# A two-layer macaron transformer trunk: where the row scale factors are spread over the partitions

## The chip, the cores and the metric

One Trainium2 chip, one of its NeuronCores. The metric is the device time of one launch in microseconds (us). Engines: PE (TensorE), DVE (VectorE), ACT (ScalarE), POOL (GpSimd), SP (SyncE, here only a queue of DMAs).

## The reference, cut to what matters

`x` is 256 tokens by 1024 features, float32. There are two layers; each is a half-step SwiGLU feed-forward (FFN), a token mixing (eight heads of sparse latent attention with an indexer and a top-64, and eight heads of forgetting attention) and a second half-step FFN:

```
for l in range(2):
    h = h + 0.5 * swiglu(rms_norm(h, ffn1_norm[l]), ffn1_gate[l], ffn1_up[l], ffn1_down[l])
    h = h + token_mixing(rms_norm(h, mix_norm[l]), w_in[l], ...)
    h = h + 0.5 * swiglu(rms_norm(h, ffn2_norm[l]), ffn2_gate[l], ffn2_up[l], ffn2_down[l])
return rms_norm(h, final_norm)
```

`rms_norm` divides each token (row of `h`) by the root of its mean square, then multiplies by a gain per feature. `swiglu(x) = (silu(x @ w_gate) * (x @ w_up)) @ w_down`, with 2816 hidden features. There are thus six normalizations inside the layers (numbered n = 0 to 5 below: n = 0, 2, 3 and 5 stand before an FFN, n = 1 and 4 before a mixing) and a seventh at the end.

## The kernel before, in words

The tokens lie as two blocks `b` of 128 on the partitions (`X`). Each block is transposed on PE (16 transposes a norm, L674), so that features lie on the partitions and tokens along the free dimension; ACT multiplies by the gain and rounds to the high part `xhi`, DVE makes the low part `xlo`. Each float32 product is made from high and low parts of both operands, in matmuls of 128x512 and 128x256. The weights come as a stream of chunks (3 units of 1024 columns each: the "front" of two units, in an FFN gate and up, and the "back" of one unit, down). SP loads them into two slots of `raw` (L246 front, L250 back) as soon as the slot's chunk before has been split; ACT rounds them to `whi`, DVE subtracts to get `wlo` (L1065, L1071; a few of these on POOL).

The row factor of a norm is not applied to `x`. The matmuls run on the gained, unnormalized `x`, and their output, which has features on the partitions and tokens along the free dimension, is multiplied by `rows`, a tile of 128 partitions by 256 tokens, in which every partition holds the same 256 row factors. It is used by DVE and, in the mixing, by POOL.

How `rows` comes about, for each of the six norms: ACT sums squares per token (L379), DVE makes the mean (`mean`, L1082), POOL raises to the power -0.5 (`power`, L297, one instruction for each block, into `rstd`, one factor per partition). DVE multiplies the identity by `rstd` into two diagonals of 128x128 (L1112). PE multiplies a matrix of ones by the two diagonals into a PSUM bank (`spread_rows`, which calls `spread`, L682), in the middle of the gate tile of the second chunk (FFN: `up(1)`) or of the first query tile (mixing: `tile(QI)`). DVE copies the bank to `rows` (L1118) and goes on. Order on DVE in `norm` (L1085): the eight `xlo`, mean of block 0, split of the first front half of the next chunk, mean of block 1, two diagonals, split of the second half, the copy.

Order on DVE behind it: in an FFN (`step(0)`) `hg` = gate * rows (L1136), `ur` (L1144), then ACT's sigmoid, `ht` (L1147), `hf` (L1159), ACT's rounding to `hhi` (L415) and `hlo` (L1161). PE's order is written out by hand: `up(0)`, `up(1)`, `down(0)`, then `up(2)`, `down(1)` and so on; `down(0)` waits for `hlo` (L729). In the mixing DVE first does `ct` = latent * rows (L1252), a copy of the small weights' projection (`wft`, L1254), the index key (L1256, two halves), the split of the back of chunk 1 (L1071), ten small operations, and, after POOL's `crstd` (L347), two diagonals for a second spread (L1276); PE does `tile(QI)`, then `tile(QI + 1)` with `token_major` (L863 and L868, which waits for `wft` and for ACT's square of `ct`) in its middle, then `tile(QI + 2)` with `latent_rows` in its middle, which spreads the latent's own factors in the same way as before (`spread`, L682) and isn't touched by the change.

All waits are semaphores set by hand; every engine runs its own instructions in order.

Of the kernel before, what the change touches and what calls it, by code (L numbers as in the profile page):

```python
# [17 lines left out]
F32 = mybir.dt.float32  # L18
F32R = mybir.dt.float32r
BF16 = mybir.dt.bfloat16  # L20
ALU = mybir.AluOpType
ACT = mybir.ActivationFunctionType

P = 128
D = 1024
S = 256
# [56 lines left out]

def trunk(nc, x, stream, gains, final_gain, consts, rel_bias, out, table):
    with ExitStack() as ctx:
# [3 lines left out]
        def sems(names):  # L89
            return [ctx.enter_context(nc.semaphore(n)) for n in names.split()]  # L90
# [83 lines left out]

        ROWS_FFN, ROWS_MIX = 2, 7
        CB = 2
# [25 lines left out]
        front_done, back_done = sems("front_done back_done")  # L202
        x_ready, ss_out, ms_out, rstd_out, diag_out, rows_mm, rows_out = sems(
            "x_ready ss_out ms_out rstd_out diag_out rows_mm rows_out")
        ones_set, nc2_set, pickr_set, ur_out, ht_out, nchi_out = sems("ones_set nc2_set pickr_set ur_out ht_out nchi_out")
# [82 lines left out]
        def _(pool):  # L288
# [4 lines left out]
            def power(n):  # L293

                for b in range(NB):
                    pool.wait_ge(ms_out, n * NB + b + 1)
                    nc.gpsimd.tensor_tensor(rstd[:, b:b + 1], ms[:, b:b + 1], mhalf[:, b:b + 1],  # L297
                                            ALU.pow).then_inc(rstd_out, 1)

            def split_front(l, m, half):  # L300

                k = NF + m
                s, at = k % 2, slice(half * UNIT, (half + 1) * UNIT)
                pool.wait_ge(w_front, chunk(l, k) * 2 + half)
                pool.wait_ge(hi_front, chunk(l, k) * 2 + (half + 1))
                nc.gpsimd.tensor_tensor(wlo[:, s, at], raw[:, s, at], whi[:, s, at].bitcast(F32),
                                        ALU.subtract).then_inc(w_front, 1)
# [32 lines left out]
            for l in range(DEPTH):  # L340
                power(l * 3)
                power(l * 3 + 1)
                if l == 0:
                    pool.wait_ge(const_in, 16)
                    nc.gpsimd.tensor_copy(pickr[:], pick).then_inc(pickr_set, 1)
                pool.wait_ge(cms_out, l + 1)
                nc.gpsimd.tensor_tensor(crstd[:, :], cms[:, :], mhalf[:, :], ALU.pow).then_inc(crstd_out, 1)  # L347
                split_front(l, 4, 0)
                scale(l, 0, 1)
                split_front(l, 4, 1)  # L350
                scale(l, 1, 2)
                split_back(l, 4)
                scale(l, 2, 3)
                split_front(l, 5, 0)
                scale(l, 3, 4)
                split_front(l, 5, 1)
                scale(l, 4, NWIDE)
                for hh in range(2 * NH):
                    share(l, hh)
                power(l * 3 + 2)  # L360
            power(DEPTH * 3)

# [234 lines left out]
        def _(pe):  # L597
# [86 lines left out]

            def spread_rows(n, bank):

                pe.wait_ge(diag_out, n + 1)
                spread(bank).then_inc(rows_mm, 1)

            def ffn(l, phase):  # L690
                k0 = phase * (NF + MIXC)

                def up(f, i=0):
# [15 lines left out]
                    for g in range(2):  # L709
# [6 lines left out]
                        for k in range(KT):  # L716
                            if f == 1 and g == 0 and k == KT // 2:
                                spread_rows(l * 3 + 2 * phase, ROWS_FFN)
                            if f == NF - 1 and g == 1:
                                t = three(ps[:, GU + 2 * s + 1, 0:S], w(s, UNIT + k * P, P), xt(k), k == 0, k == KT - 1)  # L720
                            else:
                                t = wide(GU + 2 * s + g, w(s, g * UNIT + k * P, P), k)
# [31 lines left out]
            def mix(l):  # L754
# [126 lines left out]
                u.then_inc(feat_mm, 1)  # L881
                tile(QI, front(1, 0), 0, lambda: spread_rows(l * 3 + 1, ROWS_MIX))
                tile(QI + 1, front(1), UNIT, token_major)
# [175 lines left out]
        def _(dve):  # L1059
# [24 lines left out]

            def norm(n, g, l, k, bank, first=False):  # L1085

# [21 lines left out]
                if not first:  # L1108
                    mean(n, 1)
                for b in range(NB):  # L1110
                    dve.wait_ge(rstd_out, n * NB + b + 1)
                    t = nc.vector.tensor_scalar(diag[:, b, :], ident, rstd[:, b:b + 1], None, ALU.mult)  # L1112
                t.then_inc(diag_out, 1)
                split_front(l, k, halves=(1,))
                if first:
                    split_back(l, 0)
                dve.wait_ge(rows_mm, n + 1)
                nc.vector.tensor_copy(rows[:, :], ps[:, bank, 0:S]).then_inc(rows_out, 1)  # L1118
                dve.wait_ge(rows_out, n + 1)

# [268 lines left out]
            for l in range(DEPTH):  # L1389
                norm(l * 3, G_FFN1, l, 1, ROWS_FFN, first=l == 0)  # L1390
                ffn(l, 0)
                norm(l * 3 + 1, G_MIX, l, NF + 1, ROWS_MIX)
                mix(l)
                norm(l * 3 + 2, G_FFN2, l, NF + MIXC + 1, ROWS_FFN)
                ffn(l, 1)
# [109 lines left out]
```

## Time and profile before

| what | value |
|---|---|
| median of 3 runs | 1011.92 us (1011.25 to 1012.65) |
| the profiled execution's own time | 1012.57 us |
| its span, first to last instruction | 1010.7 us |
| PE, DVE, ACT, POOL busy | 997.6, 763.0, 538.5, 124.7 us |
| granted TensorE clock, mean | 0.997 of full speed |

Times in rows are microseconds from the span's start; a row of a timeline is start, duration, engine, line, operation, output<-inputs, shapes, count, and in brackets how long the engine was idle just before and what ended that. The duration of a matmul is from issue to its modelled end, and matmuls overlap; what one adds to PE's time is read from the starts or from the chain.

### The profile page before, as it was taken

The numbers are of one execution on the slowest core, as the hardware profiler recorded it, in microseconds if no ns is written. First come the engines' busy times: TensorE is split into PE (matmuls) and PEld (weight loads), VectorE is DVE, ScalarE is ACT, GpSimd is POOL, SyncE is SP. The second block draws the span as 40 slices with busy tenths as digits, with TensorE's granted clock in tenths as the row PEclk, the third lists the DMA queues.
The fourth block names the chain that finished last, engine by engine and source line by source line (L and its number), as shares of the span: only waits on it lengthen the run. The fifth ranks groups of instructions, "written<-read, shape, count | busy, mean of one in ns | idle before, by whom it ended". The sixth has DMA issues, their size and how long they took to land.

```text
span 1010.7 us, 16529 instructions
## 1 busy us (share of the span) xinstructions
PE 997.6 (99%) x5652; PEld 846.2 (84%) x5652; DVE 763.0 (75%) x1556; ACT 538.5 (53%) x974; POOL 124.7 (12%) x148
## 2 busy tenths in 40 slices
PE   9999999999999999999999999999999999999996
PEld 8878888898878888888888888889887788888885
DVE  6868777688677877777788777777786778777775
ACT  5545555566556555555555555555755555555552
POOL 1000000018552000000000000000185400000000
PEclk9999999999999999999999999999999999999998
DMA  8786556544525665555536555554363446555541
GB/s 319 223 277 208 190 185 189 184 160 137 205 68 182 194 221 187 186 187 187 188 126 211 187 188 188 187 187 149 137 213 121 164 152 219 194 187 187 187 145 42
DMA packets 36053, 183.17 MB, mean 181 GB/s; under 512 B 3984, under 2 KB 6192, under 8 KB 21680
## 3 DMA queue, kind: packets, MB, share of 16 engines
q1 hardware_dynamic: 35632, 182.53, 54.6%
q8 instruction: 23, 0.38, 0.2%
q10 hardware_dynamic: 384, 0.15, 0.1%
q14 instruction: 14, 0.11, 0.0%
HBM read 181.61 MB, written 2.62 MB: 182 GB/s over the span
## 4 chain that ended last, share of the span: by engine, by line
PE 93%; DVE 3%; DMA 2%; ACT 1%; issue 1%; POOL 0%; POOLq 0%; DVEq 0%; SPq 0%; ACTq 0%
PE ps L606 31%; PE ps L607 16%; PE ps L600 12%; PE ps L602 12%; PE ps L601 12%; DMA raw<-stream 2%; PE ps L839 1%; PE ps L616 1%; DVE wlo L1065 1%; PE ps L674 1%; PE ps L620 1%; PE ps L617 1%; PE ps L851 1%; PE ps L830 1%; PE ps L826 1%
## 5 line engine op out<-in xcount | busy, mean ns | idle before, releaser
L606 PE MATMUL ps<-xboth,whi 128*128 128x512 f32 x1440 | 508.5, 395 | 1.5 <-DVE wlo L1065 1.5
L607 PE MATMUL ps<-xboth,wlo 128*128 128x256 f32 x1440 | 403.1, 280 | 0.0
L606 PEld LDWEIGHTS ps<-xboth,whi 128*128 128x128 f32 x1440 | 270.0, 188 | 66.0 <-DVE wlo L1065 2.1
L607 PEld LDWEIGHTS ps<-xboth,wlo 128*128 128x128 f32 x1440 | 271.9, 189 | 3.3
L1065 DVE TENSOR_TENSOR wlo<-raw,whi 128x1024 fp32r<-128x1024 f32 (+2 forms) x215 | 251.0, 1204 | 9.3 <-ACT whi L370 9.3
L370 ACT CAST whi<-raw 128x1024 fp32r<-128x1024 f32 (+1 forms) x222 | 217.5, 1029 | 14.6 <-PE ps L602 9.2
L1071 DVE TENSOR_TENSOR wlo<-raw,whi 128x1024 fp32r<-128x1024 f32 (+1 forms) x110 | 131.9, 1199 | 99.6 <-ACT whi L374 99.5
L410 ACT ACTIVATE sig<-hg 128x256 f32<-128x256 f32 x88 | 36.8, 418 | 198.6 <-DVE hg L1142 182.2
L374 ACT CAST whi<-raw 128x1024 fp32r<-128x1024 f32 (+1 forms) x112 | 112.7, 1006 | 51.7 <-PE ps L602 51.5
L600 PE MATMUL ps<-whi,hhi 128*128 128x512 f32 x352 | 139.2, 395 | 0.0
L602 PE MATMUL ps<-whi,hlo 128*128 128x512 f32 x352 | 139.1, 395 | 0.0
L601 PE MATMUL ps<-wlo,hhi 128*128 128x512 f32 x352 | 138.5, 394 | 0.0
L297 POOL TENSOR_TENSOR rstd<-ms,mhalf 128x1 f32<-128x1 f32 x14 | 13.5, 976 | 776.9 <-DVE ms L1082 776.9
L415 ACT CAST hhi<-hf 128x256 fp32r<-128x256 f32 x88 | 35.8, 406 | 97.7 <-DVE hf L1159 97.7
L602 PEld LDWEIGHTS ps<-whi,hlo 128*128 128x128 f32 x352 | 66.1, 188 | 16.1
L600 PEld LDWEIGHTS ps<-whi,hhi 128*128 128x128 f32 x352 | 66.1, 188 | 15.7
L601 PEld LDWEIGHTS ps<-wlo,hhi 128*128 128x128 f32 x352 | 66.1, 188 | 12.5
L1161 DVE TENSOR_TENSOR hlo<-hf,hhi 128x256 fp32r<-128x256 f32 x88 | 37.4, 425 | 41.6 <-ACT hhi L415 41.6
L600 PE MATMUL ps<-xboth,whi 128*128 128x256 f32 x160 | 46.4, 290 | 0.0
L601 PE MATMUL ps<-xboth,whi 128*128 128x256 f32 x160 | 45.2, 282 | 0.0
L602 PE MATMUL ps<-xboth,wlo 128*128 128x256 f32 x160 | 45.2, 282 | 0.0
L1147 DVE TENSOR_TENSOR ht<-ur,sig 128x256 f32<-128x256 f32 x88 | 37.5, 426 | 9.2
(172 smaller groups left out, 1189.6 us busy)
## 6 DMA issues: line engine op xcount, KB each, us to landing
raw<-stream SPq DMA_DIRECT2D x111, 1024.0 KB, 5.2
raw<-stream SPq DMA_DIRECT2D x114, 512.0 KB, 3.6
table<-table SPq DMA_DIRECT2D x1, 1524.0 KB
cst<-consts SPq DMA_DIRECT2D x1, 1088.0 KB, 12.8
X<-x SPq DMA_DIRECT2D x2, 512.0 KB, 5.1
bias<-table SPq DMA_DIRECT2D x1, 1024.0 KB, 10.3
out<-feat SPq DMA_DIRECT2D x4, 256.0 KB, 2.0
fgain<-final_gain SPq DMA_DIRECT2D x1, 512.0 KB, 11.2
```

Source lines behind the costliest of these rows:

```text
L370: nc.scalar.copy(whi[:, k % 2, at], raw[:, k % 2, at]).then_inc(hi_front, 1)
L374: nc.scalar.copy(whi[:, k % 2, FRONT:FRONT + used], raw[:, k % 2, FRONT:FRONT + used]).then_inc(hi_back, 1)
L410: nc.scalar.activation(sig[:, s, :], hg[:, s, :], ACT.Sigmoid).then_inc(sig_out, 1)
L600: nc.tensor.matmul(out_, a[0], b[0], start=start, stop=False)
L601: nc.tensor.matmul(out_, a[0], b[1], start=False, stop=False)
L602: return nc.tensor.matmul(out_, a[1], b[0], start=False, stop=stop)
L606: nc.tensor.matmul(ps[:, bank, :], a[0], xboth[:, k, :], start=k == 0, stop=False)
L607: return nc.tensor.matmul(ps[:, bank, 0:S], a[1], xhi[:, k, :], start=False, stop=k == KT - 1)
L1065: nc.vector.tensor_tensor(wlo[:, s, at], raw[:, s, at], whi[:, s, at].bitcast(F32), ALU.subtract).then_inc(w_front, 1)
L1071: nc.vector.tensor_tensor(wlo[:, s, at], raw[:, s, at], whi[:, s, at].bitcast(F32), ALU.subtract).then_inc(w_back, 1)
L1147: nc.vector.tensor_tensor(ht[:, s, :], ur[:, s, :], sig[:, s, :], ALU.mult).then_inc(ht_out, 1)
L1161: nc.vector.tensor_tensor(hlo[:, s, :], hf[:, s, :], hhi[:, s, :].bitcast(F32), ALU.subtract).then_inc(hlo_out, 1)
```

## The change

For each of the six norms POOL, after both powers, writes each block's 128 factors to a small DRAM tensor `rowd` (2 x 128) with a DMA from its own queue, waits until both have landed, and reads `rowd` back with a third DMA that writes all 256 factors to each of the 128 partitions of `rows`. DVE waits for that DMA where it copied. The diagonals, the matmuls with ones and the copy of these six norms are gone; `latent_rows` keeps its own.

```diff
@@ POOL
+            def rows_of(n):
+                if n:
+                    pool.wait_ge(rows_in, n * 16)
+                for b in range(NB):
+                    pool.wait_ge(rstd_out, n * NB + b + 1)
+                    pool.dma_start(rowd[b:b + 1, :].rearrange("b p -> p b"), rstd[:, b:b + 1]).then_inc(rowd_in, 16)
+                pool.wait_ge(rowd_in, (n + 1) * NB * 16)
+                pool.dma_start(rows.rearrange("p (b q) -> p b q", b=NB), rowd.unsqueeze(0).to_broadcast([P, NB, P])
+                               ).then_inc(rows_in, 16)
             for l in range(DEPTH):
                 power(l * 3)
+                rows_of(l * 3)
                 power(l * 3 + 1)
+                rows_of(l * 3 + 1)
                 if l == 0:
                     pool.wait_ge(const_in, 16)
                     nc.gpsimd.tensor_copy(pickr[:], pick).then_inc(pickr_set, 1)
...
                 power(l * 3 + 2)
+                rows_of(l * 3 + 2)
             power(DEPTH * 3)
@@ PE
-            def spread_rows(n, bank):
-                pe.wait_ge(diag_out, n + 1)
-                spread(bank).then_inc(rows_mm, 1)
...
                         for k in range(KT):
-                            if f == 1 and g == 0 and k == KT // 2:
-                                spread_rows(l * 3 + 2 * phase, ROWS_FFN)
...
-                tile(QI, front(1, 0), 0, lambda: spread_rows(l * 3 + 1, ROWS_MIX))
+                tile(QI, front(1, 0), 0)
@@ DVE, norm
-                for b in range(NB):
-                    dve.wait_ge(rstd_out, n * NB + b + 1)
-                    t = nc.vector.tensor_scalar(diag[:, b, :], ident, rstd[:, b:b + 1], None, ALU.mult)
-                t.then_inc(diag_out, 1)
                 split_front(l, k, halves=(1,))
                 if first:
                     split_back(l, 0)
-                dve.wait_ge(rows_mm, n + 1)
-                nc.vector.tensor_copy(rows[:, :], ps[:, bank, 0:S]).then_inc(rows_out, 1)
-                dve.wait_ge(rows_out, n + 1)
+                dve.wait_ge(rows_in, (n + 1) * 16)
@@ kernel
+    rowd = nc.dram_tensor("rowd", (NB, P), F32, kind="Internal").ap()
+    trunk(nc, *args, out, table, rowd)
```

## Rows read from the trace of the kernel before

**Rows 1.** The page: PE's busy time, and the chain that ended last, by engine.

```profile
PE 997.6 (99%) x5652; PEld 846.2 (84%) x5652; DVE 763.0 (75%) x1556; ACT 538.5 (53%) x974; POOL 124.7 (12%) x148
...
PE 93%; DVE 3%; DMA 2%; ACT 1%; issue 1%; POOL 0%; POOLq 0%; DVEq 0%; SPq 0%; ACTq 0%
```

**Rows 2.** The chain in order of time (start, us on the chain, what), norms 1 and 2.

```profile
207.79 0.45 PE ps L682 x4
...
328.70 0.44 PE ps L682 x4
```

**Rows 3.** The instructions on the diagonals: durations in ns min/median/max, first and last start.

```profile
L682 PE MATMUL ps<-diag,ones x32: 270/274/275, 18.6 to 824.8; 128*128 128x128 f32 x32
L1112 DVE TENSOR_SCALAR diag<-cst,rstd x12: 285/288/1040, 16.7 to 822.9; 128x128 f32<-128x128 f32 x12
```

**Rows 4.** Timeline of norm 2 (before an FFN): POOL, DVE, and PE's `down(0)`.

```profile
324.93 1.99 POOL L297 TENSOR_TENSOR rstd<-ms,mhalf 128x1 f32<-128x1 f32 x2 [15.94 <-DVE ms L1082]
...
329.18 0.42 DVE L1118 COPY rows<-ps 128x256 f32<-128x256 f32 x1 [0.80 <-PE ps L682]
329.64 0.42 DVE L1136 TENSOR_TENSOR hg<-ps,rows 128x256 f32<-128x256 f32 x1
...
332.05 0.42 DVE L1161 TENSOR_TENSOR hlo<-hf,hhi 128x256 fp32r<-128x256 f32 x1 [0.47 <-ACT hhi L415]
...
333.15 0.39 PE L600 MATMUL ps<-whi,hhi 128*128 128x512 f32 x1
```

**Rows 5.** Timeline of norm 1 (before the mixing): POOL, DVE and PE.

```profile
204.10 1.97 POOL L297 TENSOR_TENSOR rstd<-ms,mhalf 128x1 f32<-128x1 f32 x2 [186.86 <-DVE ms L1082]
...
208.73 0.42 DVE L1252 TENSOR_TENSOR hg<-ps,rows 128x256 f32<-128x256 f32 x1
...
213.61 0.48 DVE L1276 TENSOR_SCALAR diag<-cst,crstd 128x128 f32<-128x128 f32 x2 [0.81 <-POOL crstd L347]
...
211.03 0.61 PE L863 MATMUL ps<-cst,wft 16*128 16x16 f32 x4
...
215.00 0.61 PE L682 MATMUL ps<-diag,ones 128*128 128x128 f32 x4
```

**Rows 6.** Timeline of norm 0 (the first FFN): POOL, DVE and PE.

```profile
15.19 2.05 POOL L297 TENSOR_TENSOR rstd<-ms,mhalf 128x1 f32<-128x1 f32 x2 [4.45 <-DVE ms L1082]
...
20.20 0.42 DVE L1136 TENSOR_TENSOR hg<-ps,rows 128x256 f32<-128x256 f32 x1
...
23.22 0.43 PE L600 MATMUL ps<-whi,hhi 128*128 128x512 f32 x1
```

**Rows 7.** DMA issues: count, KB each, median us to landing; then one line's issue times.

```profile
raw<-stream SPq DMA_DIRECT2D x111, 1024.0 KB, 5.2
raw<-stream SPq DMA_DIRECT2D x114, 512.0 KB, 3.6
...
out<-feat SPq DMA_DIRECT2D x4, 256.0 KB, 2.0
...
L283 SPq DMA_DIRECT2D out<-feat x4: 332/338/348, 1005.7 to 1008.2; - x4
...
cst<-rel_bias ACTq DMA_DIRECT2D x1, 1.0 KB, 6.3
```

**Rows 8.** POOL's instructions that write the row factors, ns min/median/max.

```profile
L297 POOL TENSOR_TENSOR rstd<-ms,mhalf x14: 542/772/1529, 15.2 to 1005.8; 128x1 f32<-128x1 f32 x14
```

**Rows 9.** SP's queue around norm 2.

```profile
328.56 0.33 SPq L246 DMA_DIRECT2D raw<-stream  x1
```

**Rows 10.** Busy time by stretch; the last three columns: granted clock, DMA share, GB/s.

```profile
15.00:18.00 3.00, 3.00 (x22) 2.43 (x21) 2.32 (x7) 1.57 (x3) 2.05 (x2) 1.00 1.03 428
...
1004.00:1005.00 1.00, 0.00 (x0) 0.00 (x0) 0.26 (x2) 1.00 (x2) 0.55 (x1) 1.00 0.00 0
1005.00:1006.00 1.00, 0.00 (x0) 0.00 (x0) 1.00 (x3) 0.14 (x2) 0.23 (x1) 0.57 0.00 0
```

**Rows 11.** Timeline of PE at the end: its last matmul.

```profile
1002.45 0.39 PE L602 MATMUL ps<-whi,hlo 128*128 128x512 f32 x1
```

More of the change, by code:

```diff
@@ L81, with trunk @@
 NC = C_E + NH * P
-def trunk(nc, x, stream, gains, final_gain, consts, rel_bias, out, table):
+def trunk(nc, x, stream, gains, final_gain, consts, rel_bias, out, table, rowd):
     with ExitStack() as ctx:
@@ L173, in trunk @@
         GU = 4
-        ROWS_FFN, ROWS_MIX = 2, 7
         CB = 2
@@ L202, in trunk @@
         front_done, back_done = sems("front_done back_done")
-        x_ready, ss_out, ms_out, rstd_out, diag_out, rows_mm, rows_out = sems(
-            "x_ready ss_out ms_out rstd_out diag_out rows_mm rows_out")
+        x_ready, ss_out, ms_out, rstd_out, rowd_in, rows_in = sems(
+            "x_ready ss_out ms_out rstd_out rowd_in rows_in")
         ones_set, nc2_set, pickr_set, ur_out, ht_out, nchi_out = sems("ones_set nc2_set pickr_set ur_out ht_out nchi_out")
@@ L1083, in mean, with norm @@
                                         ).then_inc(ms_out, 1)
-            def norm(n, g, l, k, bank, first=False):
+            def norm(n, g, l, k, first=False):
                 if first:
@@ L1389, in _ @@
             for l in range(DEPTH):
-                norm(l * 3, G_FFN1, l, 1, ROWS_FFN, first=l == 0)
+                norm(l * 3, G_FFN1, l, 1, first=l == 0)
                 ffn(l, 0)
-                norm(l * 3 + 1, G_MIX, l, NF + 1, ROWS_MIX)
+                norm(l * 3 + 1, G_MIX, l, NF + 1)
                 mix(l)
-                norm(l * 3 + 2, G_FFN2, l, NF + MIXC + 1, ROWS_FFN)
+                norm(l * 3 + 2, G_FFN2, l, NF + MIXC + 1)
                 ffn(l, 1)
@@ L1501 @@
     table = nc.dram_tensor("table", (NH, P * TAB), F32, kind="Internal").ap()
-    trunk(nc, *args, out, table)
+    rowd = nc.dram_tensor("rowd", (NB, P), F32, kind="Internal").ap()
+    trunk(nc, *args, out, table, rowd)
     r = run_bass_kernel_spmd(nc, [arrays], core_ids=[0])
```

## The prediction

> **What bounds the kernel now.** I read the page's busy times first, then the chain of work that ended last, then the timeline around the norms, then the DMA issues. PE is busy 99% of the span, and 93% of the chain lies on it [rows 1]. So the kernel is bound by PE's stream of matmuls, nearly without holes, and a change can act in two ways only: it takes instructions out of that stream, or it makes PE wait where it now doesn't. What the other engines do is free as long as it is ready when PE comes to it. The timeline around a norm shows how closely that holds: in norm 2 the last operand for `down(0)`, `hlo`, is finished at 332.47, and PE starts on it at 333.15, 0.68 us later [rows 4]. That small margin is what the change is to be held against.
>
> **What is removed.** The four PE records of one spread (two matmuls, each in two passes) hold the chain for 0.45 us [rows 2]; of the 32 records [rows 3] 24 go (six norms), 8 stay with `latent_rows`. Gain if nothing else moves: 6 x 0.45 = 2.7 us. On DVE 12 diagonals of 0.29 us [rows 3] and six copies of 0.42 us [rows 4] go, 6.0 us in all. I cost these at nothing by themselves: PE's stream hides them, and the copy stands only in the wait for `rows`, which is priced whole below. The splits that stood behind the diagonals come about 1 us earlier, so SP's next front load too (at 328.56 in norm 2 [rows 9]); PE needs neither earlier.
>
> **What is added.** Three DMAs on POOL's queue in each norm, of which two steps follow each other: both writes must have landed before the read is issued, and the read must have landed before DVE goes on. DVE runs in order, so everything behind that wait waits too: in an FFN `hg`, `ur`, `ht`, `hf`, `hlo` and the splits of the next chunks, and through them ACT's sigmoid and PE's `down(0)`; in a mixing `ct`, but also `wft` and the split of chunk 1's back, which don't need `rows` at all. Behind the DMAs on POOL stand only the copy to `pickr` (used much later) and `crstd`, which comes after `ct` anyway: nothing. SP's queue is not passed.
>
> Call L the time from the end of the second power on POOL to DVE's first use of `rows`.
>
> - Norm 2 (FFN): the powers end at 324.93 + 1.99 = 326.92. From the start of `hg` (329.64) to the end of `hlo` (332.47) are 2.83 us [rows 4]; with 0.05 us for the semaphore PE can start `down(0)` at 326.92 + L + 2.88, and it started at 333.15. The delay is L - 3.35. Norms 3 and 5 have the same pattern and the same constant within 0.02.
> - Norm 0: powers end at 17.24, `down(0)` at 23.22 [rows 6], the steps between as long: L - 3.10.
> - Norm 1 (mixing): powers end at 206.07. From the start of `ct` (208.73) to the end of the latent's diagonals (213.61 + 0.48 = 214.09) are 5.36 us, and PE spreads them at 215.00 [rows 5]. Delay: 206.07 + L + 5.36 + 0.05 - 215.00 = L - 3.52. Norm 4 is the same. (The earlier stop, at `token_major` at 211.03 [rows 5], is inside this one: `wft` ends 0.88 us after `ct` starts, and that wait is shorter.)
>
> The delay is counted against the old schedule, so the 0.45 us of the removed spread is in it: where L is under some 2.9 us the term is -0.45, never less. Can PE make a delay good? No: it has no holes later to give up [rows 1]. Sum over six: 6L - (3.10 + 3 x 3.35 + 2 x 3.52) = 6L - 20.2 us. Break-even is L = 3.4 us.
>
> **The size of L.** No DMA of POOL's queue is in this trace, and none so small that can be timed apart, so it is bounded from other rows.
>
> - Issue: an issue holds SP's queue 0.33 us [rows 7]; the nearest work on POOL itself, powers of one element per partition, take 0.54 to 1.53, median 0.77 us [rows 8]. I take 0.77, a row of the engine that will issue them, over one of SP's queue. Three: 2.3 us. Ends: 3 x 0.33 = 1.0 and 3 x 1.53 = 4.6.
> - Write: the four output stores of 256 KB land in 2.0 us, in a quiet time [rows 7]. Ends: 2.0 (a smaller one may land a little sooner, no row shows it) and 3.6, the stream's 512 KB. I take 2.0.
> - Read back: 2.0 to 3.6 likewise; the stream's load of 1024 KB, 5.2 us to landing, is in flight at that time [rows 7, 9]. I take 2.6, nearer the quiet one because it is 128 KB in all.
> - Two semaphores: 0.1 us.
>
> L = 2.3 + 2.0 + 2.6 + 0.1 = 7.0 us. The sum is 6 x 7.0 - 20.2 = +21.8 us. In norm 0 the initial loads still fill the DMA engines up to 18 us (share 1.03 [rows 10]), and the writes are issued from 17.3 on: +1.0. Total +22.8 us; 1012.57 + 22.8 = 1035.4 us for a profiled execution, which stood 0.65 us above the median before, so 1034.7.
>
> **The rivals.**
>
> *Quicker transfers.* The landing time is counted from the issue, so the issues of the row may be inside it, and only the second write's issue comes on top: L = 0.33 + 2.0 + 2.0 + 0.1 = 4.4, sum +6.2, 1018.1 by the median. For it: the two store rows; against it: they are from SP's queue, and the one small transfer here took 6.3 us [rows 7], though in the crowded start. The Trainium skill, "DMA: Bandwidth & Descriptors", Anatomy of one DMA, fits a GpSimd DMA at about 2.0 us fixed plus its bytes, set-up within; by it two steps would be an estimated 4.0 us and the sum near +4, and its Specifications give the GpSimd path a later first byte than the sync path (about 1 against 0.6 us), which points the other way.
>
> *Slow transfers.* Both steps land like the stream's 512 KB, 3.6 us, because they share the 16 DMA engines with it: L = 2.3 + 7.2 + 0.1 = 9.6, sum +37.4, 1049.3. For it: a front load is under way in each of norms 2 to 5, and a write in pieces of 4 bytes is of a kind no row shows.
>
> *The clock falls in the stalls.* With L = 7.0 PE comes to `down(0)` at 332.70 and goes on at 336.80, 4.1 us idle. At the end of this trace the granted clock went from 1.00 to 0.50 inside the stretch 1005 to 1006 (mean 0.57, so at about 1005.1 [rows 10]), 2.3 us after PE's last matmul ended at 1002.84 [rows 11]; that is from 2.4 to 1.2 GHz. If it falls in each stall and stays down as long as the stall was, PE loses half of 4.1 us six times, +12 us: 1047. Against it: it is one case, and the price rests on how long the clock would stay down, which no row shows. The Trainium skill, "TensorE: Matmul & The Clock Gate", says that an idle PE is halved and must be busy for a while to get the clock back; this trace agrees as to the fall, at 0.57, and shows no return.
>
> *Faster.* All three transfers and their issues within 2.9 us: `rows` then comes as early as today, PE is never late, and the six spreads are gained: -2.7 us, 1009.2. It decides at L = 3.4. Against it: two landings in a row, each no quicker than any landing shown here, are 4.0 us alone.
>
> **How the numbers follow.** 0.2% is 2 us, about what can be told from no change. Chances: the forecast (L from 5 to 8.5, clock up) 0.54; quicker transfers 0.14; slow transfers 0.11; the clock 0.16; faster 0.03; L within 0.35 us of break-even, no visible change, 0.02. The low end takes in the quicker transfers, the high end the slow ones and the clock: 1017 to 1053. The forecast's own range, L from 5.1 (all low ends) to 8.5: 1023 to 1044. The ends all taken high together (L = 11.9) lie outside. Faster 0.03, same 0.02, slower 0.95.
>
> **What would show it.** PE should idle once before L729's matmuls (`down(0)`) in four norms, some 4 us each, and before L863 or the latent's L682 in two; its busy time should fall by about 2.7 us and the span grow all the same. DVE should be idle ahead of `hg` and `ct`, released by a DMA into `rows`, about 7 us after the second power. POOL's queue should show 18 issues. The splits of the next chunk should end about 1 us earlier. If the wait ahead of `hg` is under 2 us or ends before PE needs it, the forecast is wrong; if PE's granted clock shows 0.5 behind the stalls, the third rival is there.

## The result and the profile after

The changed kernel takes 1098.6 us (median of 4 runs, 1098.3 to 1100.1) against 1011.6 us (4 runs) before: ratio 1.086 [1.0845, 1.088], 87 us slower. The forecast was 1034.7 us with a range from 1017 to 1053. The direction was right, the size was short by a factor of nearly four, and the time lies far outside the range.

The page of the changed kernel: busy time by engine, the chain that ended last by engine, and one row of the DMA issues (count, KB each, median us to landing); the last row is from the view of the DMAs.

```profile
PE 1008.9 (92%) x5628; PEld 854.4 (78%) x5628; DVE 756.4 (69%) x1538; ACT 538.8 (49%) x974; POOL 139.5 (13%) x166
...
PE 84%; DMA 8%; DVE 4%; POOL 1%; ACT 1%; issue 1%; POOLq 0%; DVEq 0%; SPq 0%
...
rows<-rowd POOLq DMA_DIRECT2D x6, 128.0 KB, 4.2
...
rowd<-rstd POOLq DMA_DIRECT2D x12, 0.5 KB, 9.0
```

Against [rows 1] PE has 24 records fewer and is busy 11 us longer, and DMAs, which held 2% of the chain, now hold 8%. So two things happened: PE stands still, and some of its matmuls take longer. The table of waits (who waited for whom: us in total, times, longest us) tells the first.

```profile
DVE hg L1136 <- DMA rows<-rowd: 63.1, 4, 17.2
POOL rows L307 <- DMA rowd<-rstd: 58.9, 6, 11.3
...
PE ps L613 <- DVE hlo L1161: 53.3, 4, 15.8
...
DVE hg L1252 <- DMA rows<-rowd: 30.4, 2, 15.3
...
PE ps L869 <- DVE wft L1254: 23.7, 2, 11.9
```

POOL waits 58.9 us for the six pairs of writes, some 10 us each, and in the same time DVE waits for `rows`. PE waits 53.3 us in the four FFNs and 23.7 us in the two mixings, 77.0 us in all. In the mixings PE stops at `token_major` alone (L869, which was L863); no wait is shown at the latent's spread. Lines have moved: `down(0)` is now L613 to L615, and the powers are at L296.

The chain in order of time through norm 2 (start, us, what) has the whole path from the second power to PE.

```profile
353.90 1.52 POOL rstd L296 x2
355.42 1.10 issue
356.52 0.60 POOL rowd L305
357.12 9.59 DMA rowd<-rstd
366.71 0.28 issue
367.00 4.26 DMA rows<-rowd
371.28 0.43 DVE hg L1136
...
373.69 0.43 DVE hlo L1161
374.26 0.77 PE ps L613
375.03 0.43 PE ps L614
...
380.13 0.23 PE ps L619
```

The second of the two writes, of 512 bytes each, is 9.59 us on its way, and the read back 4.26 us. What the prediction called L is 371.28 - 356.57 = 14.7 us here (the powers end at 353.90 + 2.67). By the same two ends it is 16.3, 14.7, 14.7, 14.9, 14.9 and 15.0 us in norms 0 to 5, 90.5 us in all. The last rows show the second thing: PE's matmuls take 0.43 us a piece until 379.7 and 0.23 us from then on. The busy time by stretch (length; PE, PEld, DVE, ACT, POOL; granted clock, DMA share, GB/s) says why.

```profile
362.00:364.00 2.00, 0.00 (x0) 0.00 (x0) 0.00 (x0) 0.00 (x0) 0.00 (x0) 1.00 0.00 0
...
366.00:368.00 2.00, 0.00 (x0) 0.00 (x0) 0.00 (x0) 0.00 (x0) 0.55 (x1) 0.52 0.00 0
...
378.00:380.00 2.00, 2.00 (x8) 1.59 (x7) 1.83 (x6) 0.68 (x2) 0.00 (x0) 0.57 1.02 256
380.00:382.00 2.00, 2.00 (x14) 1.74 (x13) 1.10 (x3) 1.26 (x2) 0.00 (x0) 1.00 0.85 340
```

PE ends its last matmul before the stall at 361.92. The clock stands at 1.00 for about four more microseconds, falls to 0.50 (from 2.4 to 1.2 GHz) at about 366, and is back at about 379.7, some 5.4 us after PE started again at 374.26. The other norms show the same with other lengths: the stalls are 11.7 to 15.8 us, and after them PE runs 3.0 (norm 0), 5.3, 5.4, 4.0, 5.9 and 5.4 us at the low clock, 29 us in all. At half speed these cost up to 14.5 us. Between 362 and 364 the DMA engines show a share of 0.00 although POOL is still waiting for its writes (the load of the stream, issued at 356.33, has landed at 362.0), so by the profile it is not a lack of bandwidth that keeps them.

The sum from the after side: 77.0 us of idle PE, less 2.7 us for the spreads that are gone, leaves 87.0 - 74.3 = 12.7 us of the difference of the spans (1097.7 - 1010.7) for the clock. PE's busy time gives nearly the same: it grew by 11.3 us although 2.7 us of spreads are gone, 14.0 in all. Both lie just under the upper bound of 14.5.

### The profile page after: what moved, and what is told of

It reads as the page before. It is cut to its first block, busy times and chain, and to the rows that moved or that the text cites. A ratio compares the mean times of both kernels' runs of the same rounds, so it can differ in the third digit from the quotient of the medians.

```text
span 1097.7 us, 16486 instructions
## 1 busy us (share of the span) xinstructions
PE 1008.9 (92%) x5628; PEld 854.4 (78%) x5628; DVE 756.4 (69%) x1538; ACT 538.8 (49%) x974; POOL 139.5 (13%) x166
## 4 chain that ended last, share of the span: by engine, by line
PE 84%; DMA 8%; DVE 4%; POOL 1%; ACT 1%; issue 1%; POOLq 0%; DVEq 0%; SPq 0%
PE ps L619 29%; PE ps L620 15%; PE ps L613 12%; PE ps L615 11%; PE ps L614 11%; DMA rowd<-rstd 6%; DMA rows<-rowd 2%; DVE xboth L1104 2%; POOL rstd L296 1%; PE ps L845 1%; PE ps L857 1%; DVE X L1124 1%; PE ps L836 1%; DMA raw<-stream 1%; PE ps L832 1%
## 5 line engine op out<-in xcount | busy, mean ns | idle before, releaser
L383 ACT CAST whi<-raw 128x1024 fp32r<-128x1024 f32 (+1 forms) x222 | 217.6, 1029 | 13.7 <-PE ps L615 8.8
L613 PE MATMUL ps<-whi,hhi 128*128 128x512 f32 x352 | 142.9, 406 | 53.3 <-DVE hlo L1161 53.3
L615 PE MATMUL ps<-whi,hlo 128*128 128x512 f32 x352 | 142.1, 404 | 0.0
L614 PE MATMUL ps<-wlo,hhi 128*128 128x512 f32 x352 | 141.6, 402 | 0.0
L613 PEld LDWEIGHTS ps<-whi,hhi 128*128 128x128 f32 x352 | 68.1, 193 | 70.5 <-issue 54.5
L296 POOL TENSOR_TENSOR rstd<-ms,mhalf 128x1 f32<-128x1 f32 x14 | 19.2, 1380 | 786.7 <-DVE ms L1088 786.7
L615 PEld LDWEIGHTS ps<-whi,hlo 128*128 128x128 f32 x352 | 67.9, 193 | 16.8
L613 PE MATMUL ps<-xboth,whi 128*128 128x256 f32 x160 | 47.9, 300 | 0.0
L614 PE MATMUL ps<-xboth,whi 128*128 128x256 f32 x160 | 46.7, 292 | 0.0
L615 PE MATMUL ps<-xboth,wlo 128*128 128x256 f32 x160 | 46.6, 291 | 0.0
```

The source lines that it names most:

```text
L383: nc.scalar.copy(whi[:, k % 2, at], raw[:, k % 2, at]).then_inc(hi_front, 1)
L613: nc.tensor.matmul(out_, a[0], b[0], start=start, stop=False)
L614: nc.tensor.matmul(out_, a[0], b[1], start=False, stop=False)
L615: return nc.tensor.matmul(out_, a[1], b[0], start=False, stop=stop)
```

## The experiments

Three things were open: why a write of 512 bytes takes 9.6 us (theory P: by the shape of its pieces, 4 bytes each side by side in DRAM; theory Q: by POOL's queue; or the weight stream beside it), what the low clock costs, and whether anything besides the wait for `rows` costs time.

**probe** is the kernel before, with small DMAs timed one by one on POOL's queue beside the stream (p), on POOL's queue after the output is stored (q), and on SP's queue after that (s).

```
+ one:   dr[0:1, :] as a column <- rstd[:, 0:1]   128 pieces of 4 B, side by side
+ pair:  both blocks, as the change does it
+ both:  dr[128, 2] <- rstd[:, :]                 128 pieces of 8 B, side by side
+ apart: dr[128, 128][:, 0:1] <- rstd[:, 0:1]     128 pieces of 4 B, 512 B apart
+ wide:  dr[128, 128] <- ones                     128 pieces of 512 B
+ few:   16 pieces of 4 B; line: one piece of 512 B; then the read back
```

> The kernel before, untouched in its path, with small DMAs timed by themselves, two of each form: from POOL's queue while the first FFN runs and the weights stream in (p...), from POOL's queue after the last output store has landed (q...), and from SP's queue after that (s...). Forms: 128 pieces of 4 bytes (one), two such DMAs issued back to back (pair), 128 pieces of 8 bytes (both), 128 pieces of 4 bytes with 512 bytes from one to the next in DRAM (apart), 128 pieces of 512 bytes (wide), 16 pieces of 4 bytes (few), one piece of 512 bytes (line), and the read back of 256 values to 128 partitions (from ...pair to lg). In the changed kernel a pair takes 7.5 to 11.6 us to landing and the read about 4.2. Theory P (small pieces written to DRAM are slow): one 6 to 8 us on every queue and in the quiet too, wide, few and line near 2 to 3. Theory Q (POOL's queue is slow to start): every form on POOL's queue, line and wide too, over 5 us, and one on SP's queue about 2. Theory S (the weight stream holds the small DMA up): one 8 us while the stream runs, about 2 to 3 on both queues in the quiet. If the pieces hinder each other because they fall into the same stretch of DRAM, apart is clearly quicker than one.

The chain of the probe in its quiet part on POOL's queue:

```profile
1026.29 7.88 DMA qone<-rstd
...
1059.17 3.10 DMA qboth<-rstd
...
1066.20 1.69 DMA qapart<-rstd
...
1070.59 1.80 DMA qwide<-ones
...
1078.54 1.53 DMA qline<-ones
...
1082.16 3.23 DMA lg<-qpair
```

Each form was timed twice; the second times differ by less than 0.5 us. The same 128 pieces of 4 bytes take 7.9 us where they lie side by side and 1.7 us where they lie 512 bytes apart; pieces of 8 bytes side by side take 3.1. So it is neither the number of pieces (128 in `apart` and `wide` too) nor their size alone, but small pieces next to each other. On SP's queue, each write issued when the one before had landed (start, us from the first issue to the end of the second, in the timeline of the probe):

```profile
1089.31 7.52 SPq L229 DMA_DIRECT2D sone<-rstd  x2
...
1129.64 1.75 SPq L229 DMA_DIRECT2D sapart<-rstd  x2
```

An issue is 0.33 us of it, so one write of `one` takes 7.2 us there, and one of `apart` 1.4: POOL's queue is not the cause. Nor is it that the two are cut up in different ways: the view of the DMAs gives both the same 144 packets of under 512 bytes on the same queue. The busy time by stretch (columns as above), the first `one` from SP, then an `apart`:

```profile
1090.00:1091.00 1.00, 0.00 (x0) 0.00 (x0) 0.00 (x0) 0.00 (x0) 0.00 (x0) 0.50 0.08 1
1091.00:1096.00 5.00, 0.00 (x0) 0.00 (x0) 0.00 (x0) 0.00 (x0) 0.00 (x0) 0.50 0.00 0
...
1130.00:1131.00 1.00, 0.00 (x0) 0.00 (x0) 0.00 (x0) 0.00 (x0) 0.00 (x0) 0.50 0.08 1
```

The engines' records show the same work for both, done within a microsecond; for `one` five more microseconds follow in which no packet is shown and the write has still not landed. So the time that adjacency costs lies behind the last packet. Beside the stream `one` lands in 8.5 to 11.1 us and `apart` in 4.0 to 4.8: by the medians the stream adds 1.7 us to the one and 2.5 to the other. The read takes 3.2 us in quiet and 3.7 to 4.0 beside the stream.

**act_queue** moves the three DMAs of each norm to ACT's queue.

```diff
-                    pool.wait_ge(rstd_out, n * NB + b + 1)
-                    pool.dma_start(rowd[b:b + 1, :].rearrange("b p -> p b"), rstd[:, b:b + 1]).then_inc(rowd_in, 16)
+                    act.wait_ge(rstd_out, n * NB + b + 1)
+                    act.dma_start(rowd[b:b + 1, :].rearrange("b p -> p b"), rstd[:, b:b + 1]).then_inc(rowd_in, 16)
```

> The changed kernel with the three DMAs of each norm issued from ACT's queue, at a place where ACT has nothing to do. Theory Q: from the second power to DVE's first use of the rows falls from about 15 us to 5 or 6, and the time from 1098 to about 1030. Theory P: it stays within 2 us of what it is (the time within 15 us of 1098). Theory S: the same as P.

It takes 1135.6 us (2 runs, 1134.8 to 1136.3), ratio 1.122 [1.120, 1.1245], 37 us slower than the change itself, which neither expectation had. The timeline of norm 2, ACT's queue, SP's and DVE:

```profile
367.39 1.47 ACTq L382 DMA_DIRECT2D rowd<-rstd  x2
385.26 0.33 ACTq L384 DMA_DIRECT2D rows<-rowd  x1
...
368.26 0.33 SPq L245 DMA_DIRECT2D raw<-stream  x1
...
389.71 0.42 DVE L1136 TENSOR_TENSOR hg<-ps,rows 128x256 f32<-128x256 f32 x1 [21.63 <-DMA rows<-rowd]
```

The writes are out at 367.4 to 368.9 and the read is issued only at 385.3: they land 16 to 17 us after they were issued, beside one load of the stream. Theory Q falls: it wanted some 1030 us. Why they take longer here than from POOL's queue is open: from 366 to 374 the DMA engines show a share of 0.60 to 0.94 while they move 25 to 35 GB/s, but no run separates the causes.

**no_wait** keeps all 18 DMAs and lets nothing on DVE wait for them: the read goes into a tile that isn't used at that time, and the kernel leaves the factors out (`rows` is all 1.0). In a mixing POOL waits for the read ahead of its own splits.

```diff
-                pool.dma_start(rows.rearrange("p (b q) -> p b q", b=NB), rowd.unsqueeze(0).to_broadcast([P, NB, P])
+                pool.dma_start(rback.rearrange("p (b q) -> p b q", b=NB), rowd.unsqueeze(0).to_broadcast([P, NB, P])
...
-                dve.wait_ge(rows_in, (n + 1) * 16)
+                dve.wait_ge(rstd_out, (n + 1) * NB)
```

> The changed kernel with the six spreads removed and the three DMAs issued as in it, but the read back lands in a tile that nobody uses, and the factors in rows are left out (all 1.0). If the whole loss is the wait for the rows, the time is that of the kernel before less the six spreads, 1009 us (1008 to 1010), and the granted clock is back at 0.997. If the DMAs or the longer powers on POOL cost something by themselves (contention with the stream, splits held up), it is over 1013.

1027.4 us (1022.9 to 1030.5), ratio 1.014 [1.011, 1.0165]: 71 us of the 87 are the wait of DVE and what it brings, and 16 remain, where the main expectation had none; its other case, over 1013 if the DMAs cost something by themselves, holds. The waits of this kernel name two causes.

```profile
DVE diag L1278 <- POOL crstd L360: 14.8, 2, 7.8
...
PE ps L697 <- DVE diag L1278: 11.2, 2, 5.9
ACT whi L385 <- DMA raw<-stream: 11.1, 3, 5.5
```

POOL's timeline at norm 1 shows how the first comes about.

```profile
210.73 1.12 POOL L306 DMA_DIRECT2D rowd<-rstd  x2
221.84 0.54 POOL L308 DMA_DIRECT2D lg<-rowd  x1 [9.99 <-DMA rowd<-rstd]
...
223.37 0.73 POOL L360 TENSOR_TENSOR crstd<-cms,mhalf 128x2 f32<-128x2 f32 x1
```

POOL runs in order. While it waits 10 us for its own writes, `crstd` waits behind them, the latent's diagonals behind `crstd`, and PE 5.9 us behind those. And ACT waits 11.1 us for loads of the stream, against 3.9 in the next kernel: the 512 KB load that SP issues 3.2 to 4.8 us behind the writes lands after 9.4 to 11.0 us in norms 1 to 5, and after 3.4 to 4.1 in the next kernel.

**no_wait_spaced** is the same with pieces 512 bytes apart (the row that is read was written once at the start, by one more DMA).

```diff
-                    pool.dma_start(rowd[b:b + 1, :].rearrange("b p -> p b"), rstd[:, b:b + 1]).then_inc(rowd_in, 16)
+                    pool.dma_start(spaced[b, :, 0:1], rstd[:, b:b + 1], allow_slow_non_contiguous=True).then_inc(rowd_in, 16)
```

> The kernel of no_wait (nothing on DVE waits for the rows, factors left out) with the writes spaced 512 bytes apart in DRAM. no_wait took 1027 us where the removals alone should give 1009; I put that to the writes: POOL is held until they land and so comes late to crstd, on which PE waits in the mixing (two times 5.6 us), and the front load issued beside them lands in 10 to 16 us in place of 5.2. If so, with writes that land in 4 to 5 us both are gone: 1009 to 1013 us. If any DMA traffic beside the stream costs this, it stays over 1020.

1009.8 us (10 runs), ratio 0.9978 [0.9966, 0.9989]. With DMAs of the same number and size in each norm, on the same queue, the 18 us between the two kernels are the adjacency of the pieces. POOL's wait fell from 64.0 to 26.9 us, and PE's wait for the diagonals is gone; the waits:

```profile
POOL lg L310 <- DMA spaced<-rstd: 26.9, 6, 4.8
```

**no_spread** has the removals alone: no spreads, no diagonals, no copies and no DMAs. It leaves the factors out too (`rows` is all 1.0), and DVE waits only for the powers.

```diff
-                rows_of(l * 3)
...
-                rows_of(l * 3 + 1)
...
-                rows_of(l * 3 + 2)
```

> The change's removals alone: the diagonals, spreads and copies of the six norms gone, no DMA and no wait in their place, and the factors in rows left out (all 1.0). Expected: 6 x 0.45 = 2.7 us less than before, 1009.2 us; DVE's 6 us are worth nothing. If DVE's work was in the way after all, it is 1006 or less; if the spreads were hidden, 1012.

1009.15 us (10 runs) against 1011.82 us, ratio 0.9973 [0.9963, 0.9982]: -2.7 us. Both kernels without a wait end near 1009: it is what the change could have gained at best. The 2.7 us are what PE's six spreads were priced at, so DVE's six microseconds are worth nothing that can be told.

**spaced** is the changed kernel, waits included, with the write of no_wait_spaced. What it reads back is the row of ones from the start, so it leaves the factors out, but the path in time is whole.

> The changed kernel with the factors written to a tensor in which each 4-byte piece has 512 bytes of DRAM to itself; the read back takes two contiguous rows of ones instead, so the factors in rows are left out (1.0). Same number of pieces, same sizes, same queue, same waits. By the timed DMAs a pair of such writes should land in about 5 us where the change's takes 10.2, and the read stays at 4.2: five us less in each norm, some 30 less in all, and less of the clock's fall: 1055 to 1070 us. If not the shared stretch of DRAM but the stream or the number of pieces decides, it stays over 1085.

1063.0 us (2 runs, 1061.7 to 1064.4), ratio 1.051 [1.0485, 1.0527]: 35.6 us less than the change, from the placing of the written bytes. In norm 2 the write takes 5.17 us for 9.59, and the read behind it, of a row that was written long before, 3.17 for 4.26. The waits:

```profile
DVE hg L1138 <- DMA rows<-rowd: 36.8, 4, 9.7
POOL rows L309 <- DMA spaced<-rstd: 25.8, 6, 4.9
```

Even with the quickest write of a column that was found here, the detour costs 51 us.

**one_write** sends both blocks with one DMA, 128 pieces of 8 bytes, and lets DVE copy the row into order.

```diff
-                for b in range(NB):
-                    pool.wait_ge(rstd_out, n * NB + b + 1)
-                    pool.dma_start(rowd[b:b + 1, :].rearrange("b p -> p b"), rstd[:, b:b + 1]).then_inc(rowd_in, 16)
+                pool.wait_ge(rstd_out, n * NB + NB)
+                pool.dma_start(rowd, rstd[:, :]).then_inc(rowd_in, 16)
...
+                nc.vector.tensor_copy(rows.rearrange("p (b q) -> p q b", b=NB),
+                                      hf[:, 1, :].rearrange("p (q b) -> p q b", b=NB)).then_inc(rows_out, 1)
```

> The changed kernel with one write of 128 pieces of 8 bytes (both blocks' factors of a token) in place of two writes of 128 pieces of 4 bytes; the read back gives them interleaved, and DVE puts them in order with one copy of 0.42 us. Timed alone, the 8-byte form took 3.2 us in the quiet and 8.1 beside the stream, the pair 7.5 and about 10 to 11. Expected: 1.5 to 3 us less in each norm, 1080 to 1090 us. If the pieces' number in one 512-byte stretch is all that counts (64 in place of 128, in the same time), the same.

1076.8 us (2 runs), ratio 1.064 [1.062, 1.066], 22 us less than the change and some 3 us below the expected range: the write lands 5.9 us after its issue (median).

**sbuf_row** turns the column into a row inside SBUF first, then writes the row as one piece of 1 KB and reads it back: one more step, but no small pieces side by side in DRAM.

```diff
+                    pool.dma_start(hf[0:1, 1, b * P:(b + 1) * P], rstd[:, b:b + 1]).then_inc(rowd_in, 16)
...
+                pool.dma_start(rowd.rearrange("b p -> (b p)").unsqueeze(0), hf[0:1, 1, :]).then_inc(line_in, 16)
```

> The changed kernel with a step more: the two columns of factors are written into one row of an SBUF tile (128 pieces of 4 bytes each, side by side), that row goes to DRAM as one piece of 1 KB, and then the read back as before. If small pieces side by side are slow only in DRAM, the first step lands in 2 to 4 us and the second in 2 to 4.6: no slower than the change in spite of one more DMA, 1075 to 1095 us. If 4-byte pieces are slow into any memory, the first step is about 10 us as before and the second comes on top: 1120 or more.

One run of 1075.8 us, with these waits of POOL:

```profile
POOL rowd L307 <- DMA hf<-rstd: 28.5, 6, 5.4
...
POOL rows L309 <- DMA rowd<-hf: 8.0, 6, 1.3
```

Two steps, 28.5 + 8.0 = 36.5 us, are quicker than the one step of 58.9 us. The pieces are 4 bytes and side by side in this kernel too, only in SBUF, and cost half: what is dear is adjacency in DRAM. The read back takes 3.3 us (median) here, and it is the same read of a row that was just written.

**held** lets SP issue the front load of the stream that falls beside a norm's DMAs only after the read has landed.

```diff
+                    if s and n is not None:
+                        sp.wait_ge(rows_in, (n + 1) * 16)
```

> The changed kernel, in which SP issues the front load that falls beside the three DMAs of each norm only after the read back has landed. By the timed DMAs the quiet is worth about 2 us on the pair of writes (7.5 in place of 10) and 0.5 to 1 on the read (3.2 in place of 4.2); six times 2.5 to 3 us: 1080 to 1084 us, and the load itself is early enough still. If the stream has no part in the slow writes, the time stays at 1098; if the later load comes too late for ACT's next split, it rises.

1083.5 us (4 runs), ratio 1.071 [1.069, 1.073], as expected: the stream's load beside the writes costs some 15 us, 2.5 a norm. All of it is in the writes: the read, for which 0.5 to 1 us had been expected, lands in 4.4 us (median), no sooner than in the change. POOL's wait for the writes goes from 58.9 to 42.3 us:

```profile
POOL rows L314 <- DMA rowd<-rstd: 42.3, 6, 7.7
```

**power_first** makes DVE wait for both powers ahead of its second split, as the diagonals made it do before the change.

```diff
+                dve.wait_ge(rstd_out, (n + 1) * NB)
                 split_front(l, k, halves=(1,))
```

> The changed kernel with one more wait on DVE: the split of the second half starts only when both powers on POOL are done, as it did before the change (there the diagonals stood between). In the changed kernel the second power ended 0.65 us later after its mean than before (2.67 in place of 1.99 us for the pair) and in norm 0 2.3 us later. If that is DVE's split in the way of POOL, the pair is back at 2.0 us and the time falls by 5 x 0.65 + 1 to 2 = 4 to 5 us, to 1094; if not, the time stays or rises.

1089.2 us (4 runs), ratio 1.075 [1.072, 1.078], 9.4 us less than the change where 4 to 5 were expected. Norm 2 on POOL after the change:

```profile
353.90 2.67 POOL L296 TENSOR_TENSOR rstd<-ms,mhalf 128x1 f32<-128x1 f32 x2 [15.95 <-DVE ms L1088]
```

The same in this kernel, with SP's load of the stream:

```profile
350.24 1.99 POOL L296 TENSOR_TENSOR rstd<-ms,mhalf 128x1 f32<-128x1 f32 x2 [15.95 <-DVE ms L1088]
352.25 1.14 POOL L305 DMA_DIRECT2D rowd<-rstd  x2
...
353.67 0.33 SPq L245 DMA_DIRECT2D raw<-stream  x1
```

The powers take 1.99 us again, as in [rows 4]; that is 5.7 us over the six norms. The rest goes with the order of the DMAs: here the writes go out 1.4 us ahead of the stream's load, while in the changed kernel the load is out at 356.33 and the first write at 356.52. POOL's wait for the writes is 47.7 us in place of 58.9. But the load and the read pay for it: in norms 1 to 5 the load lands after 12.1 to 12.5 us, where it took 4.8 to 5.7 issued 0.2 us ahead of the writes, and the read, with the load still under way, takes 5.1 us (median) for 4.2. In sum L is 85.5 us for 90.5.

**warm** puts 64 matmuls that nobody reads into the stall of each FFN, to keep the clock up.

```diff
+                for _ in range(64):
+                    nc.tensor.matmul(ps[:, 2, 0:S3], nc2[:, 0:P], nc2[:, :], start=True, stop=True)
```

> The changed kernel with 64 matmuls of 128x384 into an unused bank between up(1) and down(0) of the four FFN norms, about 10.5 us of work in the 12.3 us that PE waits there. If the clock's fall costs what the trace suggests (5.4 us at half speed behind each stall, 2.7 us lost), the time falls by about 4 x 2.7 = 11 us, to 1088, and the clock stays at 1.00 behind these four norms. If the clock has no part, it stays at 1098 or rises where the matmuls outlast the wait.

1091.5 us (2 runs, 1090.1 to 1092.9), ratio 1.079 [1.077, 1.081]: 7 us less than the change, not 11. In three of the four norms it worked, in norm 0 it didn't. A stretch of norm 0 and one of norm 2, columns as above:

```profile
40.00:44.00 4.00, 2.24 (x5) 1.82 (x6) 2.90 (x5) 3.25 (x5) 0.00 (x0) 0.50 0.00 0
...
374.00:378.00 4.00, 3.47 (x17) 2.80 (x16) 2.90 (x5) 3.16 (x5) 0.00 (x0) 1.00 0.01 4
```

In norm 0 the writes of this run were slower (POOL waited 14.7 us, DVE 20.3), the filling matmuls ended at 34.0, and PE stood 7.7 us before `down(0)`. Three norms at 2.7 would be 8 us. So the low clock is a cost of its own, on top of the wait.

**merged** leaves the change aside: the kernel before, with each spread as one matmul of 256 columns.

```diff
-                for b in range(NB):
-                    t = nc.tensor.matmul(ps[:, bank, b * P:(b + 1) * P], ones[:, :], diag[:, b, :], start=True, stop=True)
-                return t
+                return nc.tensor.matmul(ps[:, bank, 0:S], ones[:, :], diag[:, :, :].rearrange("p b q -> p (b q)"),
+                                        start=True, stop=True)
```

> The kernel before with each spread as one matmul of 256 columns in place of two of 128 on the same ones: the same result in half the instructions, eight spreads (six of the norms, two of the latent). The chain gives 0.45 us to the four records of a spread; two records of 256 columns should take 2 x 0.11 = 0.22 to 0.3. Expected: 8 x 0.15 to 0.2 = 1.2 to 1.8 us less than before, about 1010.3 us.

1011.08 us (11 runs) against 1011.48 us, ratio 0.9993 [0.9982, 1.0005]: no difference that can be told, and not the 1.2 to 1.8 us that were expected. One spread on the chain:

```profile
327.29 0.43 PE ps L681 x2
```

Two records for four, and 0.43 us for the 0.44 to 0.45 of [rows 2]: for these two shapes the f32 matmul goes by its columns, not by the number of instructions.

No kernel that still computes the factors beat the one before.

## Why the prediction was right and wrong

**The bound and the structure held.** PE's stream had no slack to give: the delay per norm was taken as L less a constant, the sum as 6L - 20.2. With the measured L it gives 90.5 - 20.2 = 70.3, and with the later end of the powers (below, 5.7) 76.0; measured are 77.0 of idle PE less 2.7, 74.3. PE stopped where the forecast said, before `down(0)` in four norms and at `token_major` in two. One small step was off here: for the mixings the sum took the latent's spread (L - 3.52) and held the stop at `token_major` to be the shorter one. By the rows it is L - 4.03 there (206.07 + 0.88 + 0.05 against 211.03), 0.5 us a mixing less, and in the changed kernel PE waits there and not at the spread: 1.0 of the 1.7 us between 76.0 and 74.3.

**The removals held.** The spreads' 2.7 us are what no_spread gained, and what DVE lost was worth nothing.

**The step that failed is the write: "I take 2.0."** Its upper end was 3.6. It took 9.59 us in norm 2. The rows from which both ends were taken, 256 KB stores and the stream's loads [rows 7], are of long pieces; the prediction wrote that "a write in pieces of 4 bytes is of a kind no row shows" and put that sentence under a rival, with a price of 3.6, instead of into the upper end. By the probe (8.1 less 1.9 in quiet) and by spaced (a median landing of 4.6 us) some 4.4 to 6.2 us of the write are the pieces' adjacency, by held some 2.5 us are the stream's load beside it, and about 2 us are left (`apart` in quiet takes 1.9), which is what was forecast. The Trainium skill, "DMA: Bandwidth & Descriptors", Anatomy of one DMA, gives about 2.0 us fixed whatever the size: the probe agrees for 512-byte pieces (1.8), for one piece (1.5) and for 4-byte pieces 512 bytes apart (1.7 to 2.1), and disagrees for those side by side (7.9 to 8.3). Its Specifications say that transfers under 512 B are done as a read, a modification and a write. No run looks inside the memory, but the size alone doesn't explain the times, since `apart` has the same 4 bytes in the same 144 packets and is quick; rewriting one stretch of 512 bytes again and again would fit them, and so would a wait for the writes to neighbouring bytes, but neither was shown: no distance between 4 or 8 and 512 bytes was tried.

**The read was sized too low**, 2.6 for 4.2 us. The quiet time is already 3.2, so the four stores were the wrong row for it as well. The other microsecond is not the stream here: in norm 2 no load is under way during the read (SP issues at 356.33, landed at 362.0, and then at 376.02), and in held, with the load kept back, it is 4.4. It goes with the small pieces side by side: where the row was written in another way, in spaced and sbuf_row, the read takes 3.2 and 3.3 us. Why is open.

**The issues were a little too dear**: three at 0.77 = 2.3 us, while the chain has 0.60 for the first write and 0.28 ahead of the read, and the read's issue lies within its 4.26 us.

Sized right, L would have been 0.6 + 9.6 + 0.3 + 4.3 = 14.8 where the sum had 7.0. Over six norms these 7.8 us make 47 of the 64 us that were missing, and norm 0 adds 0.5 (1.5 longer than the others, where the forecast had 1.0). With 5.7 for the powers and 12.7 for the clock, both below, that is 66 for 64, and the mixings' 1.0 goes off it.

**"The splits of the next chunk come about 1 us earlier; PE needs neither earlier"** was right for PE and wrong for POOL. The diagonals had kept DVE waiting for both powers; without them its second split (two inputs from SBUF) runs beside the second power, and two powers take 2.67 us for 1.99: 0.68 us later in five norms and 2.3 in norm 0 (2.05 before, [rows 6], 4.32 after), 5.7 us in all. It also brought the stream's load, 1.2 us earlier against the powers, as forecast, ahead of the writes. power_first undid both and gained 9.4 us. The Trainium skill, "SBUF — State Buffer", Who interferes with whom, has this: a DVE instruction with two SBUF inputs contends with a GpSimd instruction that reads SBUF; the powers' times agree.

**"Behind the DMAs on POOL stand only the copy and `crstd`: nothing."** In the changed kernel it costs nothing, since what `crstd` is made of comes from DVE after `rows`. It is a wait of its own all the same: no_wait shows it as 11.2 us on PE.

**The clock rival came true**, together with slow transfers, not in their place. Its price, +12 us "if it stays down as long as the stall was", came out near the 12.7 us left over from the spans, but that is luck: its rule was half of a stall of 4.1 us, while the stalls are 11.7 to 15.8 us and PE's time at the low clock behind them is 3.0 to 5.9 us, not as long as the stall. The error was to hold the two rivals as alternatives with a chance each. The slow case means a longer stall, so it should have carried the clock too: with L at 9.6 the stall is 6.7 us by the same sum, and by the prediction's own price, half of it six times, the slow case would have been 1049 + 20 = 1069 (an estimate). The upper end of all terms together was left out as well.

## What to carry to other kernels

A column with one element per partition that goes to DRAM side by side cost 7 to 8 us in quiet and about 10 beside a stream, and moving it to another queue did not help (up to 17 us from ACT's); leave 512 bytes between the pieces, turn the column in SBUF, or best keep to a matmul against a diagonal, here 0.45 us of PE. Where a change adds a DMA of a shape that no row of the trace shows, don't take its price from rows of large transfers: the range has to be wide upwards, and everything that a longer wait brings with it (the low clock, work queued behind it) belongs to the same case. An instruction removed from an engine that isn't the bound can still matter if its wait kept two engines apart.

## What the runs showed of the hardware that was not expected

- 128 pieces of 4 bytes to DRAM: 7.9 to 8.3 us side by side, 1.7 to 2.1 us at 512 bytes apart; of 8 bytes side by side 3.1 to 3.4 us; 16 pieces of 4 bytes side by side 1.6 us. On SP's queue 7.2 us against 1.4 from one to the next, with the same 144 packets in both, and no packet in the last five microseconds of the 7.2.
- Such writes hold up a load that is issued behind them, and hardly one that is ahead. Issued 0.2 us ahead of them (the changed kernel, norms 1 to 5), a load of the stream landed in 4.8 to 5.7 us, as in the kernel before (4.7 to 5.3), though in the crowded norm 0 one issued 0.5 us ahead took 13.7; issued 1.4 us behind (power_first), in 12.1 to 12.5 us. A load of 512 KB 3.2 to 4.8 us behind took 9.4 to 11.0 us in no_wait and 3.4 to 4.1 in no_wait_spaced. In act_queue the DMA engines moved 25 to 35 GB/s at a share of 0.60 to 0.94 beside such writes.
- A read of the row by all 128 partitions took 3.8 to 4.5 us behind two such writes (the changed kernel), and 3.1 to 3.5 us in spaced and sbuf_row. The cause is open.
- From ACT's queue the same writes beside the same load took 16 to 17 us. The cause is open.
- After a stop of PE the granted clock stayed at 1.00 for 2.9 to 5.1 us in the six norms, and for 2.3 us at the end of the kernel before [rows 10, 11]; it came back 3.0 to 5.9 us after PE went on.
